# Two attention-type layers on one core: branch products earlier, a third place for split weights, a norm's turns moved

## The reference

```python
for l in range(2):
    h = rmsnorm(x, norm_g[l])
    c = split_columns(h @ w_in[l])
    y_a = dilated_window_attention(...) * silu(a_gate)     # kind "A"
    y_b = mla_attention(...) * silu(b_gate)                # kind "B"
    y_c = nsa_attention(...) * silu(c_gate)                # kinds "cmp", "slc", "win", added up
    y_d = stick_breaking_attention(...) * silu(d_gate)     # kind "D"
    merged = 0.0
    for i, y in enumerate((y_a, y_b, y_c, y_d)):
        gate = sigmoid(h @ w_merge[l, i] + b_merge[l, i])
        merged = merged + gate * (y @ w_branch[l, i])
    x = x + merged @ w_out[l]
return rmsnorm(x, final_norm_g)
```

## Time and profile before

| what | value |
|---|---|
| median of 3 runs | 1170.82 us (1170.23 to 1171.5) |
| the profiled execution's own time | 1171.7 us |
| its span in the profile | 1169.9 us, mean granted clock 0.997 |
| PE busy | 1131.3 us, 97% of the span |
| DVE busy | 741.8 us, 63% |
| ACT busy | 657.5 us, 56% |
| POOL busy | 49.6 us, 4% |
| first block | 0 to 612 us |
| layer 0 and layer 1 of the second block | 612 to 889, 889 to 1162 us |
| last norm and store | 1162 to 1169.9 us |

### The profile page before, as it was taken

The page is one execution under the profiler, slowest core; times in us unless marked ns, Lnnn a source line. Parts: engine busy times, 40 slices in busy tenths (PEclk is TensorE's granted clock), DMA queues, the critical chain, the costliest instruction groups (busy, mean ns, idle before and its releaser), DMA issues.

```text
span 1169.9 us, 18881 instructions
## 1 busy us (share of the span) xinstructions
PE 1131.3 (97%) x7741; PEld 982.4 (84%) x7741; DVE 741.8 (63%) x1060; ACT 657.5 (56%) x1096; POOL 49.6 (4%) x59
## 2 busy tenths in 40 slices
PE   8999999999999999999999999999999999999997
PEld 8987799998988787685767878999987888899995
DVE  5758988675999842312276657546696657454686
ACT  5568857744667841222255567456636648556553
POOL 1000000000001100000000000000010000000010
PEclk9999999999999999999999999999999999999999
DMA  9862352454578999999977454344445554435331
GB/s 341 302 209 77 139 181 74 144 180 169 179 266 301 349 379 339 387 388 387 386 279 252 144 180 145 125 156 161 142 145 166 174 181 143 145 108 217 123 131 54
DMA packets 118694, 244.19 MB, mean 209 GB/s; under 512 B 5281, under 2 KB 7489, under 8 KB 117712
## 3 DMA queue, kind: packets, MB, share of 16 engines
q1 hardware_dynamic: 113392, 228.96, 55.3%
q0 software_dynamic: 4160, 11.93, 2.9%
q10 hardware_dynamic: 1056, 2.10, 0.5%
HBM read 237.48 MB, written 9.44 MB: 211 GB/s over the span
## 4 chain that ended last, share of the span: by engine, by line
PE 71%; DVE 16%; ACT 5%; DMA 4%; issue 3%; SPq 0%; POOL 0%; DVEq 0%; POOLq 0%; ACTq 0%
PE psum L624 29%; PE psum L548 12%; DVE weights_low L424 5%; PE psum L563 4%; PE psum L1381 4%; PE psum L1371 3%; PE psum L2499 2%; PE psum L1422 2%; PE psum L2516 2%; PE psum L1361 2%; DMA arena<-pair_inputs,fetched_pairs 1%; PE psum L2436 1%; PE psum L2487 1%; DMA arena<-in_w_expert_gate 1%; DMA arena<-in_w_expert_down 1%
## 5 line engine op out<-in xcount | busy, mean ns | idle before, releaser
L424 DVE TENSOR_TENSOR weights_low<-weights_raw,weights_high 128x1024 fp32r<-128x1024 f32 (+1 forms) x276 | 332.6, 1235 | 142.1 <-ACT weights_high L415 141.4
L415 ACT ACTIVATE weights_high<-weights_raw 128x1024 fp32r<-128x1024 f32 (+1 forms) x276 | 285.4, 1055 | 172.2 <-PE psum L624 67.4
L624 PE MATMUL psum<-act_high,weights_high 128*128 128x256 f32 x928 | 270.2, 291 | 3.0 <-ACT arena L2536 1.7
L624 PE MATMUL psum<-act_high,weights_low 128*128 128x256 f32 x928 | 262.2, 283 | 0.0
L624 PE MATMUL psum<-act_low,weights_high 128*128 128x256 f32 x928 | 262.0, 282 | 0.0
L624 PEld LDWEIGHTS psum<-act_high,weights_high 128*128 128x128 f32 x928 | 177.3, 191 | 9.2 <-issue 4.4
L624 PEld LDWEIGHTS psum<-act_high,weights_low 128*128 128x128 f32 x928 | 177.6, 191 | 0.6 <-issue 0.5
L624 PEld LDWEIGHTS psum<-act_low,weights_high 128*128 128x128 f32 x928 | 177.4, 191 | 0.0
L548 PE MATMUL psum<-weights_high,act_high 128*128 128x512 f32 (+1 forms) x320 | 127.8, 399 | 4.0 <-DVE weights_low L424 4.0
L548 PE MATMUL psum<-weights_high,act_low 128*128 128x512 f32 (+1 forms) x320 | 124.6, 389 | 0.0
L548 PE MATMUL psum<-weights_low,act_high 128*128 128x512 f32 (+1 forms) x320 | 124.5, 389 | 0.0
(11 more groups left out here) (481 smaller groups left out, 2120.2 us busy)
## 6 DMA issues: line engine op xcount, KB each, us to landing
weights_raw<-in_w_in SPq DMA_DIRECT2D x51, 1024.0 KB, 5.1
weights_raw<-in_w_merge SPq DMA_DIRECT2D x32, 1024.0 KB, 5.1
weights_raw<-in_w_expert_gate SPq DMA_DIRECT2D x20, 1024.0 KB, 8.7
weights_raw<-in_w_expert_up SPq DMA_DIRECT2D x20, 1024.0 KB, 8.7
arena<-in_w_expert_down SPq DMA_DIRECT2D x18, 1024.0 KB, 13.4
weights_raw<-in_w_expert_down SPq DMA_DIRECT2D x14, 1024.0 KB, 9.8
weights_raw<-in_w_out SPq DMA_DIRECT2D x12, 1024.0 KB, 5.0
arena<-in_w_expert_gate SPq DMA_DIRECT2D x12, 1024.0 KB, 11.3
```

The lines of the kernel that those rows point to most:

```text
L415: nc.scalar.activation(hi_tile(i)[:, half_at(part, n)], raw_tile(i, n)[:, cols], ACT.Copy)\
L424: dve.tensor_tensor(lo_tile(i)[:, half_at(part, n)], raw_tile(i, n)[:, cols], hi_tile(i)[:, half_at(part, n)].bitcast(f32), ALU.subtract). ...
L624: last = pe.matmul(pair(g)[:, s * SEQ:(s + 1) * SEQ], b[:, k * 512 + s * P:k * 512 + (s + 1) * P], a[:, 4 * h + k, :], start=(h == 0 and k ...
```

## The change

Five things move, all in the two layers.

1. The branch tiles of y_a and y_b (branches 0 and 1) are loaded between the gates 11 and 12, and their four products are taken inside the two slc attentions, where the gates 12 and 13 stood. The gates 12 and 13 go to win, the gates 14 and 15 behind the last attention. y_a, y_b are turned at the start of cmp's first group, y_d in slc's first, y_c behind gate 14, in blocks of their own.
2. A third place in the ring (the slots of `xn_high` and `weights_low_third`) for the tiles from 32 of one layer to 15 of the next, which are split three ahead.
3. The additions of the branches are all DVE's (`add_part`), one behind each `gated`; POOL's part is gone.
4. `feed(13)` in the D attention is gone from ACT and DVE (tile 15 has the third place), and for the gates 9 and 11 the tanh eviction stands between the two halves of the split.
5. The turn of the first row half of layer 1 stands inside the last token rows of layer 0's `out_tiles`; in both layers the turn of the second row half stands between the eight high and the four low products of the first row half's second tile. On DVE the first four of eight low parts stand ahead of the second row half's additions, and tile 2 is split ahead of the second half's turn on ACT and DVE.

The core of the diff:

```diff
         def ring_slot(i):
+            n = i - T_LAYERS
+            if n >= RING_FROM or 0 <= n < RING_TO:
+                return (2, 0, 1)[(n - RING_FROM) % L_TILES % 3]
...
@@ token_rows
+                    if k == 1 and between is not None:
+                        between()
...
                     one(k, q)
+            if between is not None:
+                between()
             pe.wait_ge(turned_lo, 4 * turn + 2 * t + h + 1)
...
+        def gate_block(b):
+            return b + (8 if b < 5 else 9 if b < 6 else 14)
+        def branch_block(half, br):
+            return 16 + 2 * half + br if br < 2 else 20 + 2 * half + br
+        def ahead(n):
+            return 3 if n + 3 < RING_TO or n >= RING_FROM - 2 else 4 if n in (W_CMP - 2, W_CMP - 1) else 2
...
-                 [(G[10], 0, 3)], [(G[11], 0, 2)], [(G[12], 0, 2)], [(G[13], 0, 2)], [(G[14], 0, 2)], [(G[15], 0, 2)]]
+                 [("turn", 0, 1), (G[10], 0, 3)], [(G[11], 0, 2)], [("turn", 3), ("branch", 0, 0)], [("branch", 1, 0)],
+                 [(G[12], 0, 2)], [(G[13], 0, 2)]]
...
-                   [(G[12], 2, 4)], [(G[13], 2, 3), (G[13], 3, 4)], [(G[14], 2, 4)], [(G[15], 2, 3), (G[15], 3, 4)]]
+                   [("branch", 0, 1)], [("branch", 1, 1, 0, 2), ("branch", 1, 1, 2, 4)],
+                   [(G[12], 2, 4)], [(G[13], 2, 3), (G[13], 3, 4)]]
@@ layer_pe
+            if l == 0:
+                turn_rows_pe(pe, k, xn, 0)
             for t in range(NT):
-                turn_rows_pe(pe, k, xn, t)
                 for i in range(2):
-                    token_rows(pe, TB + i, BB, i, t, act_hi, act_lo, r, rb, turn=k, rows=3 + 2 * l)
+                    token_rows(pe, TB + i, BB, i, t, act_hi, act_lo, r, rb, turn=k, rows=3 + 2 * l,
+                               between=(lambda: turn_rows_pe(pe, k, xn, 1)) if (t, i) == (0, 1) else None)
...
+            filler(G[14])
+            turn_branches(2)
+            filler(G[15])
             for half in range(2):
-                for br in range(4):
...
+                for br in (2, 3):
+                    branch_product(half, br)
@@ layer_act
-            def feed_gate(n):
-                feed(gate_tile(n))
+            def feed_gate(n, last_half=True):
+                early = n in (9, 11)
+                feed(gate_tile(n), (0,) if early else (0, 1))
                 if n % 2:
...
+                if early and last_half:
+                    feed(gate_tile(n), (1,))
...
             copies(2, 0)
-            feed(13)
             for g in (5, 6):
@@ layer_dve
+            gated(0, 2)
+            add_part(0, 2)
+            gated(0, 3)
+            add_part(0, 3)
+            gated(1, 2)
+            merged_low(0)
+            add_part(1, 2)
+            gated(1, 3)
+            feed(W_LATE)
+            add_part(1, 3)
...
                 norm_dve(dve, l + 3, 0)
-                low(dve, TB, r + L_TILES)
+                low(dve, TB + 1, r + L_TILES)
+                turn_rows_dve(dve, k + 2, act_hi, act_lo, NGAIN, 0, range(4))
```

More of the change, by code:

```diff
@@ L476, in turn_rows_act, with turn_rows_dve @@
                     last.then_inc(turned_hi, 1)
-        def turn_rows_dve(dve, k, hi, lo, gain, t):
-            for c in range(NC):
+        def turn_rows_dve(dve, k, hi, lo, gain, t, chunks=range(NC)):
+            for c in chunks:
                 if c % 4 == 0:
@@ L551, in token_tile, with token_rows @@
                 half_used(last, k)
-        def token_rows(pe, i, g, h, t, a_hi, a_lo, r=0, rb=0, halves=2, c0=0, turn=None, rows=None):
+        def token_rows(pe, i, g, h, t, a_hi, a_lo, r=0, rb=0, halves=2, c0=0, turn=None, rows=None, between=None):
             n = tiles[i][1]
@@ L2324, in filler, with step @@
                     n = G.index(i)
-                    feature_tile(pe, TB + i, BB + B_GATE + n // 2, n % 2, act_hi, act_lo, r, rb, k0, k1)
+                    feature_tile(pe, TB + i, BB + gate_block(n // 2), n % 2, act_hi, act_lo, r, rb, k0, k1)
+            def step(what, *parts):
+                if what == "turn":
+                    turn_branches(*parts)
+                elif what == "branch":
+                    branch_product(*parts)
+                else:
+                    filler(what, *parts)
             def turn_heads(b, srcs, width):
@@ L2527, in feed @@
             def feed(n, parts=(0, 1)):
-                high(act, TB + n + (4 if n in (W_CMP - 2, W_CMP - 1) else 2), r, parts)
+                high(act, TB + n + ahead(n), r, parts)
             def evict(g):
@@ L2680, in copies, with turned_high @@
                 nc.scalar.activation(pTs[0:keys, :], bank(6)[0:keys, :], ACT.Copy).then_inc(l_copied, 1)
+            def turned_high(*brs):
+                for b in brs:
+                    act.wait_ge(turned, 4 * k + 4 + TURN_ORDER[b] + 1)
+                    for cc in range(2):
+                        last = nc.scalar.activation(mid_hi[:, 2 * b + cc, :], turned_at(b, cc), ACT.Copy, scale=0.5)
+                    last.then_inc(turned_hi, 1)
             exps(0)
@@ L2965, in begin, with turned_low, free, gated @@
                 arguments(g, *GROUPS_L[g], steps)
+            def turned_low(*brs):
+                for b in brs:
+                    dve.wait_ge(turned_hi, 4 * k + 4 + TURN_ORDER[b] + 1)
+                    for cc in range(2):
+                        last = dve.scalar_tensor_tensor(mid_lo[:, 2 * b + cc, :], turned_at(b, cc), 0.5,
+                                                        mid_hi[:, 2 * b + cc, :].bitcast(f32), ALU.mult, ALU.subtract)
+                    last.then_inc(turned_lo, 1)
+                if brs[0] != 2:
+                    dve.wait_ge(turned_lo, 4 * k + 4 + TURN_ORDER[brs[-1]] + 1)
+                    dve.nop().then_inc(block_free[(BB + B_TURN[brs[0]]) % 2], 1)
+            def free(block):
+                g = BB + block
+                dve.wait_ge(block_free[g % 2], g // 2 + 1 + rb)
+            def gated(half, br):
+                g = BB + branch_block(half, br)
+                gate = gates[:, 2048 * br + 1024 * half:2048 * br + 1024 * half + 1024]
+                free(gate_block(2 * br + half))
+                dve.wait_ge(tile_used, halves_of(TB + branch_tile(half, br), r) + br % 2 + 1)
+                dve.scalar_tensor_tensor(merged_part(half, br), gate, 1.0, pair(g), ALU.add, ALU.mult)\
+                    .then_inc(block_free[g % 2], 1)
+            def add_part(half, br):
+                m = merged_part(half, 0)
+                free(branch_block(half, br))
+                own.wait()
+                added = dve.tensor_tensor(m, m, merged_part(half, br), ALU.add)
+                if br == 3:
+                    added.then_inc(merged_ready, 1)
+                else:
+                    own.done(added)
             feed(0)
```

242 lines of the change are left out of this document (132 added, 110 removed).

## The result

The changed kernel takes 1162.4 us (median of 4 runs, 1161.89 to 1165.03), the kernel before 1171.16 us in the same comparison: a ratio of 0.9925, 95% interval [0.9911, 0.9938], 8.8 us less. The forecast was 1164.3, 6.6 less, in a range of 1161.5 to 1168.5; the likeliest case's own range, 1162.5 to 1166, is missed by 0.1. The profiled execution of the changed kernel took 1162.77 us, with a span of 1161.0.

What follows compares the result with a forecast made beforehand. PE, busy 1131.3 of 1169.9 us, was taken as the bound, so only its pauses could give time. Terms -4.4 - 1.8 - 0.9 - 0.9 + 1.4 = -6.6 us gave a median of 1164.3 us, range 1161.5 to 1168.5.

Steps and rivals of the forecast that it cites:

- The ends of the layers: End of each layer, w_out tiles: all four PE losses to late DVE low parts go, -2.2 us a layer, -4.4 us.
- If the close one is missed: Layer ends: if the first half's merged low part is late by a us, the gain is -2.4 us instead of -4.4.
- The entry into layer 1: Border of the layers: three pauses costing 3.1 us shrink to 1.3, -1.8 us; bounds -3.1 and -0.9.
- The entry into layer 0: Start of layer 0: the third pause goes, covered by four low products, -0.9 us; bounds 0 and -1.05.
- The split taken out of D: D's second group: without the split, ACT's table load ends 0.44 us earlier in each layer, -0.9 us; bounds 0 and -1.9.
- New waits in the attentions: cmp and slc: two new pauses of 0.35 us a layer for tanh evictions, +1.4 us; bounds 0 and 4.0.
- DVE's 9.4 us at no cost: cmp, slc and win: 9.4 us of added DVE work a layer fits in 23 us idle, costing nothing.
- rival of missed margins: Attentions: margins of 0.2 to 0.8 us are missed, 2 us a layer, giving 1168.3 us; chance 0.15.
- the slower one: Attentions: DVE's in-order queue holds up PE, 1183 us if all 9.4 us a layer were waited for; chance 0.08.
- the turn that hides nothing: w_out rows: ACT or DVE is late for the turn, only -0.9 of the entry stays, 1165.7 us; chance 0.10.
- the additions on DVE's path: Layer ends: POOL's former additions lie on DVE's path, 2 x 1.22 us a layer, 1169.2 us; chance 0.05.
- More goes: Half-clock stretch after layer 0's first pauses (1.3 us) not met and new waits covered (1.4): 1161.6 us; chance 0.10.

Runs made afterwards that it cites:

- e6: Kernel before with POOL's two additions a layer left out, so one branch is missing from the sum: 3.5 us below before, ratio 0.997.
- e3: Changed kernel with the turn of layer 1's first row half back behind the last w_out rows: 1.3 us above the changed kernel, ratio 0.9941 to before.
- e5: Kernel before with the moved turns and DVE's four-low-parts order alone, the ring keeping two places: 0.6 us below before, ratio 0.999.
- e1: Kernel before with POOL's two additions a layer given to DVE in the old order: 1.3 us above before, ratio 1.001.
- e2: Kernel before with tile 15's split on DVE in the D attention moved behind the means: 0.9 us below before, ratio 0.9991.
- e4: Changed kernel with the tanh evictions of gates 9 and 11 back behind both split halves: 5.1 us above the changed kernel, ratio 0.9969 to before.
- e7: Changed kernel with one more DVE instruction of 1.2 us ahead of each of slc's four gate products in each layer: ratio 0.9969 to before.
- e9: Changed kernel with three ACT instructions in D (evictions of blocks 5 and 6, second group's first copy) ahead of splits: 1.1 us above it, 0.9935 to before.
- e10: Changed kernel with DVE's layer 0 entry reordered, block 5's eviction and D's second-group copy ahead of splits, block 6's eviction left: 1160.14 us, 0.9903 to before.

## Why the prediction was right, point by point

- **The ends of the layers** (-4.4): right in the mechanism, and some 0.7 too small. The changed kernel shows no pause there, e6 gives POOL's share (3.5 us with both layers), and the rest is the 0.31 and 0.24 that only the changed kernel removes; moving the branch products was not run alone, so that this rest is due to DVE's shorter queue there is read from the traces. "If the close one is missed" did not come: the first half's low part was in time. The size that was off is the price of a pause, idle time plus 0.15. PE's rows behind the pause of 877.18, in the kernel before:

```profile
877.49 0.39 PE L563 MATMUL psum<-weights_low,act_high 128*128 128x512 f32 x1
877.72 0.40 PE L563 MATMUL psum<-weights_high,act_low 128*128 128x512 f32 x1
```

  The step behind the pause is 877.49 - 877.18 = 0.31, where 0.23 is usual: another 0.08, which I did not count. It stands behind all six pauses from 864 to 900 us (0.08, once 0.11), so that a pause cost its idle time and 0.23 to 0.27, and a layer's end 2.5 us instead of 2.2.
- **The entry into layer 1** (-1.8): the term that was most too small, half of the difference between 6.6 and 8.8. The stage of w_out 0 and entry 1 lost 4.68 us; less the 1.75 of the layer's last two pauses that is 2.9. The mechanism was right for the first turn (e3) and for four low products as cover of the third pause (e5); for the second pause the split did move ahead of the turned rows, though e5 does not show that it takes a third place. Two sizes were off: by the price above the three pauses cost 3.5 us and not 3.1, and of the 1.3 us that I left standing some 0.6 is there, in steps between products that are too long by 0.17 at most. PE's, DVE's and ACT's timelines after, answering to the earlier trace rows:

```profile
883.28 1.04 PE L476 MATMUL psum<-params,arena 128*128 128x128 f32 x8
...
890.25 1.09 PE L476 MATMUL psum<-params,arena 128*128 128x128 f32 x8
891.10 1.17 PE L573 MATMUL psum<-xn_high,act_low 128*128 128x512 f32 x4
892.27 0.47 PE L573 MATMUL psum<-weights_high,act_high 128*128 128x512 f32 x1
...
889.44 0.76 DVE L465 TENSOR_SCALAR arena<-x_tokens,tiny 128x1024 f32<-128x1024 f32 x1
...
889.11 1.99 ACT L425 ACTIVATE weights_high<-weights_raw 128x1024 fp32r<-128x1024 f32 x2
891.01 2.15 ACT L484 ACTIVATE act_high<-psum,layer_params 128x128 fp32r<-128x128 f32 x8
```

  The second half's rows are scaled at 889.44 + 0.76 = 890.20, and PE turns them at 890.25: a step too long by 0.1, where I had 0.45 + 0.15. The split on ACT ends at 891.1, 0.9 us behind the scaled rows, where I had 1.05, and of the eight copies that take 2.15 from 891.01 half are done by 892.1; PE goes on at 892.27, 0.17 late, where I had 0.3 + 0.15. Three queues run forward by hand each had an error of 0.1 to 0.25, and here the errors added up.
- **The entry into layer 0** (-0.9): -0.94, and the third pause went as worked out. The pause of 1.07 for tile 1's low part, in the list after, was not in my account. It is not the change's: e1 and e2, with the old order there, have one of 1.06 in its place. In the profile before, the stretch at half the clock stood in its place; I took that for a loss of 1.3 us, when DVE's split was the bound under it.
- **The split taken out of D** (-0.9): the wait fell from 0.8 to 0.4 idle in each layer, 0.43 each. Right.
- **New waits in the attentions** (+1.4): both came, at the places named, as steps too long by 0.24 us each instead of 0.35: +1.0, the 0.4 that is left of the difference. e4 gives the 0.95 that I had put at 1.05.
- **DVE's 9.4 us at no cost**: right, and at the gate product that is shown under e7 by 0.1 us, which is in part luck: the margins I counted were 0.2 to 0.8. The rival of missed margins and the slower one were closer than their 0.15 and 0.08 say; the share of idle time, on which I leaned against the slower one, would not have kept it away: 1.2 us more ahead of four instructions cost 2.6 us a layer in a stretch where DVE is idle for a third.
- **The rivals**: the turn that hides nothing and the additions on DVE's path did not come in the changed kernel; e1 shows the second in the old order, at 1.3 us and not 4.9. "More goes" was right in its sign, for other reasons: not the clock, and not covered waits, but the price of a pause and the entry into layer 1.

## What to carry to other kernels

Where engines that work in the written order feed a full PE, an idle share told nothing about room here (e7): read the end of the instruction that releases a block against the start of the one that needs it, in the trace. An eviction or a copy that PE waits for goes ahead of a split in front of it, unless the split's own reader stands at the head of another queue; in D, e9 and e10 differ in that one instruction, for 1.26 us a layer. A pause that several causes share goes only when all are mended, so a part tried alone can measure as little (e1 1.3 us above before, e5 0.6 below). And a pause is priced by the steps between products, the one behind it included, not by its idle time.

## What the runs showed of the hardware

- A stretch of half the clock cost 0.15 us at most where DVE was the bound. In the profiles of the kernel before and of e6 PE's granted clock fell to 0.50, the level of 1.2 GHz, at the entry into layer 0, around the second of two pauses of 0.9 and 1.1 us; in those of e1 and e2, with the same order there, it did not, and PE, after the same two pauses, made a third of 1.06 us for DVE's split. The entry took 18.01 and 17.94 us with the slow clock, 17.86 and 17.88 without; with the changed order it took 17.02 with it (e3) and 17.07 without (the changed kernel). A window of e2 at that place (us, busy us of PE, PEld, DVE, ACT, POOL, then the granted clock):

```profile
616.50:620.50 4.00, 2.23 (x8) 1.34 (x8) 4.00 (x11) 2.71 (x5) 1.65 (x3) 1.00 1.05 387
```

The same window of e3, whose entry is the changed one:

```profile
616.50:620.50 4.00, 4.00 (x11) 2.93 (x12) 4.00 (x10) 3.69 (x6) 1.01 (x2) 0.57 1.06 391
```

  DVE is busy for all 4.00 us in both; PE waits in the one and works slowly in the other. The Trainium skill's sentence that the clock's transitions fall differently from run to run (TensorE: Matmul & The Clock Gate, What's actually happening) agrees with these runs. The price of 1.3 us that I gave the slow clock was about 0.1.
- POOL's addition of 128x1024 took 3.25 us where DVE's takes 1.22, and made one half of a split beside it 2.2 us longer. Without it the same split took 2.35 us for two halves (e6). Not every DVE row beside it suffered: the first addition of the layer ran beside a gate product, which reads one operand from PSUM and took its usual 1.22 us.

```profile
851.50 2.41 POOL L3111 TENSOR_TENSOR arena<-arena 128x1024 f32<-128x1024 f32 x1 [7.38 <-DVE arena L3055]
852.78 1.22 DVE L3055 SCALAR_TENSOR_TENSOR arena<-arena,psum 128x1024 f32<-128x1024 f32 x1 [1.43 <-PE psum L2516]
```

  A split reads both operands from SBUF. Why the one is held up and the other is not was not tested.
